# Two fused transformer blocks on one core: six edits to the order of matmuls, norm sums and squares

## The reference, cut to what matters

```python
def first_block(x, ...):                      # x: (1, 512, 1024) fp32
    h = rms_norm(x, norm1_g);  proj = h @ w_in          # u_a, v_a, val_b, gate_b
    a_out = gelu(u_a) * (causal mix of layer_norm(gelu(v_a)) by sgu_w, in chunks of 128)
    b_out = silu(layer_norm(conv31(val_b * sigmoid(gate_b))))
    x = x + concat(a_out, b_out) @ w_out
    h = rms_norm(x, norm2_g)
    x = x + square(relu(h @ w_ff1)) @ w_ff2             # 1024 -> 4096 -> 1024
    return rms_norm(x, final_g)
def second_block(x, ...):
    h = rmsnorm(x, g_pre_mix); proj = h @ w_in
    o_a = top-128 attention, 8 heads, its keys picked by an indexer
    o_d = rmsnorm(differential attention, 4 heads, g_diff_sub)
    y = concat(o_a, o_d) @ w_out
    x = x + rmsnorm(y, g_post_mix)
    h = rmsnorm(x, g_pre_mlp)
    y = square(relu(h @ w_up)) @ w_down
    return x + rmsnorm(y, g_post_mlp)
```

## Time and profile before

| | |
|---|---|
| median of 3 runs | 1189.8 us (1188.31 to 1191.36) |
| the profiled execution | 1191.36 us |
| its span, first to last instruction | 1189.6 us |
| PE busy, matmuls in the span | 1166.1 us, 5416 |
| DVE, ACT, POOL busy | 609.3, 291.4, 719.1 us |
| granted TensorE clock, mean | 0.994 of full speed |

### The profile page before, as it was taken

The page is one execution under the profiler, slowest core; times in us unless marked ns, Lnnn a source line. Parts: engine busy times, 40 slices in busy tenths (PEclk is TensorE's granted clock), DMA queues, the critical chain, the costliest instruction groups (busy, mean ns, idle before and its releaser), DMA issues.

```text
span 1189.6 us, 15617 instructions
## 1 busy us (share of the span) xinstructions
PE 1166.1 (98%) x5416; PEld 939.6 (79%) x5416; DVE 609.3 (51%) x983; ACT 291.4 (24%) x573; POOL 719.1 (60%) x438
## 2 busy tenths in 40 slices
PE   7999999999999999999999999999999999999996
PEld 5887778888888888888777777777788888888885
DVE  3988964440015443448789777847354001453113
ACT  5144162210002221120211356546321000211011
POOL 6979948666666666656455432225966666666661
PEclk9999999999999999999999998999999999999999
DMA  7321223323232323224333231012233232323211
GB/s 255 124 89 36 89 71 124 106 89 106 88 106 89 105 90 102 92 89 133 118 113 106 71 89 55 27 46 72 85 98 100 91 104 90 105 88 106 89 35 71
DMA packets 34319, 111.24 MB, mean 94 GB/s; under 512 B 4704, under 2 KB 4832, under 8 KB 34272
## 3 DMA queue, kind: packets, MB, share of 16 engines
q1 hardware_dynamic: 31056, 105.40, 27.0%
q10 hardware_dynamic: 3216, 5.21, 1.6%
HBM read 102.99 MB, written 2.10 MB: 88 GB/s over the span
## 4 chain that ended last, share of the span: by engine, by line
PE 89%; POOL 6%; DVE 2%; issue 1%; ACT 1%; DMA 0%; SPq 0%; DVEq 0%; POOLq 0%
PE bank L537 25%; PE bank L539 24%; PE bank L538 24%; PE bank L903 2%; PE bank L568 2%; PE bank L570 2%; PE bank L569 2%; POOL wl L395 2%; PE bank L917 1%; PE bank L654 1%; POOL ss L466 1%; POOL conv_p L470 1%; PE bank L945 1%; POOL wh L392 1%; PE bank L861 1%
## 5 line engine op out<-in xcount | busy, mean ns | idle before, releaser
L395 POOL TENSOR_TENSOR wl<-raw,wh 128x1024 fp32r<-128x1024 f32 x188 | 454.6, 2418 | 15.7
L392 POOL TENSOR_SCALAR wh<-raw 128x1024 fp32r<-128x1024 f32 x188 | 201.6, 1072 | 400.8 <-PE bank L539 279.5
L537 PE MATMUL bank<-xh,wh 128*128 128x512 f32 x776 | 308.3, 397 | 0.4 <-ACT va L1249 0.4
L539 PE MATMUL bank<-xh,wl 128*128 128x512 f32 x776 | 302.8, 390 | 0.0
L538 PE MATMUL bank<-xl,wh 128*128 128x512 f32 x776 | 302.5, 390 | 0.0
L537 PE MATMUL bank<-uh,wh 128*128 128x512 f32 x544 | 212.0, 390 | 0.8 <-POOL ul L452 0.8
L539 PE MATMUL bank<-uh,wl 128*128 128x512 f32 x544 | 211.7, 389 | 0.0
L538 PE MATMUL bank<-ul,wh 128*128 128x512 f32 x544 | 211.6, 389 | 0.0
L537 PEld LDWEIGHTS bank<-xh,wh 128*128 128x128 f32 x776 | 145.9, 188 | 45.6 <-issue 16.2
L539 PEld LDWEIGHTS bank<-xh,wl 128*128 128x128 f32 x776 | 145.8, 188 | 31.1
L1691 DVE TENSOR_TENSOR ul<-tmb,uh 128x512 f32 x64 | 122.7, 1918 | 90.2 <-ACT uh L1194 90.2
(11 more groups left out here) (264 smaller groups left out, 1286.1 us busy)
## 6 DMA issues: line engine op xcount, KB each, us to landing
raw<-wstream SPq DMA_DIRECT2D x189, 512.0 KB, 3.3
x<-xT SPq DMA_DIRECT2D x8, 256.0 KB, 6.0
out<-x SPq DMA_DIRECT2D x8, 256.0 KB, 2.1
qi<-ropey ACTq DMA_DIRECT2D x16, 64.0 KB, 2.5
qd<-ropey ACTq DMA_DIRECT2D x16, 64.0 KB, 2.1
kd<-ropey ACTq DMA_DIRECT2D x16, 64.0 KB, 2.1
qa<-ropey SPq DMA_DIRECT2D x16, 64.0 KB, 2.0
ka<-ropey SPq DMA_DIRECT2D x16, 64.0 KB, 2.0
```

The source lines that it names most:

```text
L392: nc.gpsimd.tensor_scalar(wh[c][:], raw[c][:], 1.0, 1.0, ALU.mult, ALU.mult).then_inc(high_ready, 1)
L395: nc.gpsimd.tensor_tensor(wl[c][:], raw[c][:], wh[c][:].bitcast(F32), ALU.subtract).then_inc(split_ready, 1)
L537: mm(out, wh_, mh, start=start, stop=False)
L539: return mm(out, wl_, mh, start=False, stop=stop)
```

## The change

Six edits, independent of each other:

1. At the start the lag of chunk 1 behind chunk 0 is 2 tiles instead of 4.
2. `out1_first` does all three matmuls of a head before the next head, so that the low part is waited for at each head.
3. `norm_sums(6)` stands ahead of chunk C_QI instead of behind its first three matmuls.
4. In the attention both `head_sums(2)` and `head_sums(3)` stand in step 17 ahead of its transposes, with ACT's roots ahead of its copies; the spread for head 3 stands in step 20 ahead of two pieces of the output projection.
5. `norm_sums_last` takes one moving column per block instead of 128, and four columns for epsilon instead of 512. It sums the last two squares on its own instead of the last one, so DVE adds one fewer. A matmul of 256 columns that nobody reads is put behind it.
6. In the x4 stage ACT squares all eight tiles after the last copy, and DVE adds them (`x4_square`) instead of POOL.

The rows below are PE's order around steps 16 to 18, before: L631 and L633 are `head_sums`, L903 scores, L917 transposes, L945 values.

The diff, with unchanged lines left out:

```diff
@@ -470,16 +470,6 @@
-            def x4_squares():
-
-                done = 5 * KT
-                pool.wait_ge(sq_ready, done + 2)
-                nc.gpsimd.tensor_tensor(ss[:], sq[0][:], sq[1][:], ALU.add).then_inc(sq_added, 2)
-                for k in range(2, KT):
-                    pool.wait_ge(sq_ready, done + k + 1)
-                    pool.wait_ge(sq_added, done + k)
-                    nc.gpsimd.tensor_tensor(ss[:], ss[:], sq[k % 2][:], ALU.add).then_inc(sq_added, 1)
-
             def v_shift():
@@ -507,15 +497,9 @@
-            split_rounds(last_round + 1, (C_FF2 + 3) // SLOTS)
-
-            second_round = (C_FF2 + 3) // SLOTS
-            for n in range(second_round * SLOTS, second_round * SLOTS + SLOTS):
-                split_chunk(n)
-                if n == C_FF2 + 3:
-                    x4_squares()
-
-            split_rounds(second_round + 1, CHUNKS // SLOTS)
+            split_rounds(last_round + 1, C_FF2 // SLOTS + 1)
+
+            split_rounds(C_FF2 // SLOTS + 1, CHUNKS // SLOTS)
             for n in range(CHUNKS // SLOTS * SLOTS, CHUNKS):
@@ -638,14 +622,15 @@
                 pe.wait_ge(bc_used, i)
-                mm(NB[:], ident[:], eps[:, 0:1].to_broadcast([P, S]), start=True, stop=False)
-                mean = inv[:, 0:1].to_broadcast([P, P])
-                pe.wait_ge(sq_added, count - 1)
+                mm(NB[:, 0:TB], ident[:], eps[:], start=True, stop=False)
+                pe.wait_ge(sq_added, count - 2)
                 for t in range(TB):
-                    mm(NB[:, t * P:t * P + P], ss[:, t * P:t * P + P], mean, start=False, stop=False)
-                pe.wait_ge(sq_ready, count)
-                for t in range(TB):
-                    last = mm(NB[:, t * P:t * P + P], sq[1][:, t * P:t * P + P], mean, start=False, stop=t == TB - 1)
+                    mm(NB[:, t:t + 1], ss[:, t * P:t * P + P], inv[:, 0:1], start=False, stop=False)
+                for i in range(2):
+                    pe.wait_ge(sq_ready, count - 1 + i)
+                    for t in range(TB):
+                        last = mm(NB[:, t:t + 1], sq[i][:, t * P:t * P + P], inv[:, 0:1], start=False,
+                                  stop=i == 1 and t == TB - 1)
                 last.then_inc(sums_done, 1)
@@ -687,15 +672,15 @@
-            def keep_warm(turns):
+            def keep_warm(turns, n=S):
...
                 for _ in range(turns):
-                    mm(bank[0][:], ones[:], mask[:], start=True, stop=True)
+                    mm(bank[0][:, 0:n], ones[:], mask[:, 0:n], start=True, stop=True)
...
             pe.wait_ge(consts_ready, 11)
-            several(C_GLU, (0, 1), 0, lag=4)
+            several(C_GLU, (0, 1), 0, lag=2)
             pe.wait_ge(split_ready, 3)
@@ -729,14 +714,10 @@
                 for k in range(4):
-                    pe.wait_ge(mixa_high, k + 1)
-                    ws = slice(k * 256 + o % 2 * P, k * 256 + o % 2 * P + P)
-                    mm(bank[o % 4][:], wh[n % SLOTS][:, ws], uh[:, k], start=k == 0, stop=False)
-                    mm(bank[o % 4][:], wl[n % SLOTS][:, ws], uh[:, k], start=False, stop=False)
-                for k in range(4):
                     pe.wait_ge(mixa_low, k + 1)
                     ws = slice(k * 256 + o % 2 * P, k * 256 + o % 2 * P + P)
-                    last = mm(bank[o % 4][:], wh[n % SLOTS][:, ws], ul[:, k], start=False, stop=k == 3)
+                    last = three(bank[o % 4][:], wh[n % SLOTS][:, ws], wl[n % SLOTS][:, ws], uh[:, k], ul[:, k],
+                                 k == 0, k == 3)
                 last.then_inc(chunk_done if o % 2 else first_even_done, 1)
@@ -837,11 +818,11 @@
-            def project(n, u, operand=None, hooks={}):
+            def project(n, u, operand=None):
...
                 pe.wait_ge(evacuated, E_P2 + u - 3)
-                chunk_transposed(n % SLOTS, bank[u % 4][:], xh, xl, operand=operand, hooks=hooks)
+                chunk_transposed(n % SLOTS, bank[u % 4][:], xh, xl, operand=operand)
@@ -862,7 +843,8 @@
             project(C_IDXK, 0, operand=(xl_ready, 2 * KT))
-            project(C_QI, 1, hooks={0: lambda: norm_sums(6, ss, 0, sq_added, 4 * KT, src2=ss2)})
+            norm_sums(6, ss, 0, sq_added, 4 * KT, src2=ss2)
+            project(C_QI, 1)
             norm_spread(6)
@@ -985,25 +967,23 @@
                     scores(n + 2)
-                if n in SPREAD_AT and SPREAD_AT[n] < 3:
+                if n in SPREAD_AT:
                     h = SPREAD_AT[n]
-                    pe.wait_ge(bc_used, 8 + h)
+                    pe.wait_ge(*((xl_ready, 3 * KT + 3) if h == 3 else (bc_used, 8 + h)))
                     norm_spread(8 + h)
...
                     out2_piece(piece)
+                if n == 17:
+                    head_sums(2)
+                    head_sums(3)
                 if 0 <= n < TILES:
                     turn(n)
-                if n in SPREAD_AT and SPREAD_AT[n] == 3:
-                    pe.wait_ge(xl_ready, 3 * KT + 3)
-                    norm_spread(11)
                 if n >= 1:
...
                     head_sums(n // 4 - 1)
-                if n in (16, 17):
-                    head_sums(n - 14)
@@ -1033,10 +1013,12 @@
             norm_sums_last(12, 5 * KT)
+            keep_warm(1, S // 2)
             norm_spread(12)
...
             norm_sums_last(14, 7 * KT)
+            keep_warm(1, S // 2)
             norm_spread(14)
@@ -1060,7 +1042,7 @@
                 act.wait_ge(sums_done, i)
-                A(sd[:, 0:TB], NB[:].rearrange("p (a b) -> p a b", a=TB)[:, :, 0], ACT.Sqrt).then_inc(sd_ready, 1)
+                A(sd[:, 0:TB], NB[:, 0:TB], ACT.Sqrt).then_inc(sd_ready, 1)
@@ -1305,10 +1287,10 @@
             def step(n):
+                if n == 17:
+                    head_roots(n)
                 if 0 <= n < TILES:
                     keep_turned(n)
-                if n == 17:
-                    head_roots(n)
                 if n in HIGH_AT:
@@ -1360,14 +1342,10 @@
                     keep_x4(k - 1)
-                if k >= 2:
-                    act.wait_ge(x4_kept, k - 1)
-                    square(x[:, k - 2])
-            act.wait_ge(x4_kept, KT - 1)
-            square(x[:, KT - 2])
             keep_x4(KT - 1)
-            act.wait_ge(x4_kept, KT)
-            square(x[:, KT - 1])
+            for k in range(KT):
+                act.wait_ge(x4_kept, k + 1)
+                square(x[:, k])
             norm_sd(13)
@@ -1967,12 +1945,10 @@
                 if 0 < k < KT - 1:
-                    add_square(bank[4], k == 1)
-                if k == KT - 2:
-                    add_square(bank[4], False, ss)
+                    add_square(bank[4], k == 1, ss if k == KT - 2 else None)
             norm_factor(12)
-            dve.sem_inc(sq_added, 1)
-            squares[0] += 1
+            dve.sem_inc(sq_added, 2)
+            squares[0] += 2
@@ -1996,6 +1972,19 @@
                 low_part(k, x4_bank[k % 3][:], col("pre_mlp", k))
+
+            def x4_square(k):
+
+                i = squares[0]
+                dve.wait_ge(sq_ready, i + 1)
+                if k == 0:
+                    dve.wait_ge(x4_kept, KT - 2)
+                    V.tensor_copy(bank[6][:], sq[i % 2][:]).then_inc(sq_added, 1)
+                else:
+                    dve.wait_ge(sq_added, i)
+                    V.tensor_tensor(bank[6][:] if k < KT - 1 else ss[:], sq[i % 2][:], bank[6][:], ALU.add
+                                    ).then_inc(sq_added, 1)
+                squares[0] += 1
@@ -2006,7 +1995,8 @@
                     x4_scale(k + 2)
-            squares[0] += KT
+            for k in range(KT):
+                x4_square(k)
             norm_factor(13)
@@ -2016,8 +2006,6 @@
                     add_square(ss, k == 1)
-                if k == KT - 2:
-                    add_square(ss, False)
             norm_factor(14)
...
             dve.wait_ge(bc_done, 15)
```

## The result

| | before | after |
|---|---|---|
| median of 4 executions each, same chip | 1189.05 us | 1201.55 us (1201.12 to 1203.33) |
| the profiled execution, its span | 1191.36, 1189.6 us | 1203.19, 1201.5 us |
| granted TensorE clock, mean | 0.994 | 0.987 |

The changed kernel is slower by 12.5 us, ratio 1.0105 with a 95% interval of 1.0086 to 1.0125. The forecast was 1196.0 us with a range of 1191.8 to 1200.2: the sign was right, the size is outside the range. Over 32 later executions on one chip the kernel before has a median of 1188.4 us (1187.7 to 1191.5), so the 1189.8 that the sum was added to was itself 1.4 us high.

What follows compares the result with a forecast made beforehand. PE's instructions in their order were taken to bound the kernel. Terms 1.2 + 0.1 + 0.45 + 1.2 - 0.2 + 3.0 = 5.75 us, plus 0.4 for the clock, gave 1189.8 + 6.2 = 1196.0 us, range 1191.8 to 1200.2.

Steps and rivals of the forecast that it cites:

- Edit 1, +1.2: At the start PE stands still for chunk 1's split, then runs the remaining matmuls at 0.229 us each: +1.2 us.
- Edit 2, +0.1: In out1_first two more matmuls stand behind the fourth low part; most of 0.46 us hides in a later wait: +0.1 us.
- Edit 3, +0.45: At norm_sums(6) PE waits for the second sum, which three matmuls of chunk C_QI had covered: +0.45 us.
- Edit 4, +1.2: In the attention, PE idles ahead of the second head_sums (+0.85) and the spread in step 20 (+0.38): together +1.2 us.
- Rival (b): Gathered head_sums in the attention prevent the 6.8 us half-clock stretch, so not slower: about 1192.4 us; chance 0.10.
- Edit 5, -0.2: In norm_sums_last, twice: one-column groups cost about the same as wide ones, the shorter drain gives some back: -0.2 us together.
- rival (a): The clock falls more often, at norms 12 and 14 and the start: 1197.7 to 1199.4, say 1198.7 us; chance 0.25.
- Edit 6, +3.0: Ahead of norm_sums(13) PE idles 4.1 us instead of 0.95 while DVE copies one square and adds seven: +3.0 us.
- The clock, +0.4: Allowance because low-rate work stands closer together at three places and a 1.2 GHz stretch costs up to half its length: +0.4 us.
- signs of being wrong: Wait ahead of norm_sums(13) under 2 us, one-column groups at 0.2 us, or 1.2 GHz stretches totalling under 5 or over 15 us.
- The starting point, 1189.8: The median of the kernel before, in us, to which the summed terms were added.
- rival (c): The sums behind the x4 stage are hidden, edit 6 costs only 1 us: 1193.0 us, no clear change; chance 0.05.

Runs made afterwards that it cites:

- wide: The changed kernel with the fifth edit undone alone, sums and epsilon of the last norm positions wide again; 1201.65 us in 4 executions, ratio 1.0115.
- narrow_dense: The kernel before with edit 5 alone plus unread 256-column matmuls between the groups of one-column sums at norms 12 and 14; 1192.87 us, ratio 1.0030.
- order: The kernel before with edits 2, 3 and 4 together; 1193.24 us in 5 executions, ratio 1.0039.
- after_warm: The changed kernel with unread 512-column matmuls, one in the wait at the start and four behind the x4 squares; 1197.74 us, ratio 1.0064.
- early_sums: The kernel before with edit 3 alone, norm_sums(6) ahead of chunk C_QI; 1190.15 us in 11 executions, ratio 1.0013.
- wide_warm: The changed kernel without edit 5, with unread matmuls in the waits at the start and behind the x4 squares; 1195.44 us, ratio 1.0062.
- squares_warm: The kernel before with edit 6 alone plus four unread 512-column matmuls in the wait for the sum of squares; 1191.23 us, ratio 1.0025.

## Why the prediction was wrong, step by step

- **The bound** (PE's order) was right. Every microsecond of the difference stands between two matmuls or in their pace.
- **Edit 1, +1.2:** the wait was right (1.16 us late with the filler in it, 1.24 in the profile of wide without one). What failed is the step that put the matmuls behind it at 0.229 us: in the changed kernel they came at 0.43 for 4 us. It measured +3.16 in the changed kernel, of which up to 0.5 us may be scatter of the start itself (the profile of narrow_dense, without edit 1, starts 0.45 us late), and +2.2 in the medians of edit 1 alone.
- **Edit 2, +0.1:** right. The last matmul ahead of PE's wait for the convolution results is 3.52 us late, where `norm_sums(0)` was 3.16, so the edit shows as 0.36 us; behind that wait it is gone again.
- **Edit 3, +0.45:** right in the trace (+0.60); alone it measured +1.7 in the medians (+0.5 to +2.6 by the interval).
- **Edit 4, +1.2:** right in the trace (+0.99, with idle times of 1.2 and 0.4 us against 1.4 and 0.4 forecast); alone it measured +2.4 in the medians (+0.5 to +2.7). Both profiles of the pair have the 6.8 us stretch in the attention, so its 1.95 us cancel in the +0.99. Rival (b), that gathered `head_sums` keep the clock up, didn't come: the stretch is there.
- **Edit 5, -0.2:** the group price (0.89) was right and the sign of the edit wrong: +2.9 in the trace, +2.5 alone. The forecast counted only what the sums themselves take; the 256-column matmul, which rival (a) held against a fall of the clock, didn't prevent it. That the clock is what edit 5 costs is shown by profiles only: putting the columns back as fillers (narrow_dense) gained nothing, nor did undoing the edit in the changed kernel.
- **Edit 6, +3.0:** the wait is right to 0.1 us, and so is its working; DVE's chain behind the last copy, in the changed kernel:

```profile
843.97 0.69 DVE L1982 COPY bank<-sq 128x512 f32<-128x512 f32 x1 [1.18 <-ACT sq L1059]
844.77 4.70 DVE L1985 TENSOR_TENSOR bank<-sq,bank 128x512 f32<-128x512 f32 x6
849.57 0.69 DVE L1985 TENSOR_TENSOR ss<-sq,bank 128x512 f32<-128x512 f32 x1
```

  From 843.97 to 850.26 are 6.3 us, forecast 6.2. The stretch behind it, twice as long as before, adds 1.2; in the medians of edit 6 alone 2.2 come on top of the wait, and that the typical execution of before has less of a stretch there than the profiled one is a likely reason, not a measured one.
- **The clock, +0.4:** this is the term that failed. It measured about 6 us: beyond the forecast's terms 2.0 at the start, 1.4 at norm 12, 1.2 behind x4 and 1.7 at norm 14, to the end. I allowed 0.4 us, with low-rate work at three places as the reason, and left out that each new wait could be followed by matmuls at half pace; at four places the clock was low for longer than before. Rival (a) named the mechanism and its places with a chance of 0.25 and 1198.7 us; it stopped at two more stretches of 3.4 us, where three new ones came and one grew. One of my own signs of being wrong came true: the stretches were to add up to 15 us at most, and PE was busy for 21.3 us in them. With fillers at the start and in the x4 stage the changed kernel took 3.8 us less, which ties that much of the surplus to the clock by experiment.
- **The starting point, 1189.8:** 1.4 us over the later median, which made the error look smaller than it is: against 1188.4 the changed kernel is +13.1.
- **A slip in rival (c):** 2.8 us for the rest and 1 us for edit 6 are 3.8, which gives 1193.6 and not 1193.0, just over the line at which slower begins. It moves a chance of 0.05 and not the forecast.

Three things stay open. Edit 5's price in company of the others is seen in profiles (norm 12: +1.3 with it, none without) and in no comparison of times. What decides whether a stretch comes in an execution, behind the same wait and the same records, was not found. And the sum of the parts measured alone (2.2 + 2.5 + 5.2 + 4.8 = 14.7) exceeds the 13.1 us of the whole against 1188.4; parts share the stretch in the attention, but that this is the reason was only argued.

## What to carry to other kernels

On a kernel that PE bounds, price a new wait twice: once as idle time, and once as the matmuls behind it at half clock, here 1.1 and 2.4 us more in the medians for waits of 1.7 and 4.0 us. The second price isn't paid in each execution, so one profile can miss it. A wait that can't be avoided is filled with matmuls into a free bank: that took 1.1 us off edit 1 (within the noise by itself), 2.4 us off edit 6 and 3.8 us off the changed kernel without touching any dependency. In the one case where the fillers lay on the path (narrow_dense) they didn't pay. Thinning out a reduction to one column per group saves PE nothing when its weight loads set the pace (0.89 us for eight records at 1 or at 128 columns), and in three of the four profiles of norm 12 that have such sums the clock fell behind them; the fourth has fillers between them.

## What the runs showed of the hardware that I had not expected

- The clock fell behind waits as short as 0.4 us when one-column records followed (behind `norm_sums(6)`, 0.38 us and sixteen records), and not in each execution: the profiles of order and after_warm have it there, those of the changed kernel, early_sums, wide and wide_warm have not. One profile is then a sample: the mean granted clock of each execution beside its time told more, as in the run where the profiled execution had 0.996 and most others 0.990 to 0.993. It doesn't count the start, though: the profile of edit 1 alone has a mean of 0.998 and matmuls 0.43 us apart until 15.5.
- One-column sums at half clock take 1.70 us for eight records, twice the 0.89 at full clock, though they hold almost no columns: the lower clock slows the weight loads as well (0.33 us for one in the stretch of squares, 0.19 at the same place in squares_warm).
- A filler of 256 columns costs 0.52 us on the path, where I had expected 0.22: the profile lists it as two records, each with a weight load. The filler of 512 columns in a wait took 0.43 us a record.
